# Threading a triangular inverse between tiles of a projection, with its predicated copies over half the columns

## The reference

```
a   = where(strict, (kb @ k.T) * lmask, 0)
t   = triangular_solve(a + eye, eye, lower, unit_diagonal)
u   = t @ (v * beta);   wk = t @ (kb * exp(gc))
# then four chunks in order:
v_new = u_c - w_c @ state
o     = qd_c @ state + a_c @ v_new
state = state * exp(gl_c) + ks_c.T @ v_new
```

## Time and profile before

| | us |
|---|---|
| median of three runs | 1038.01 (1037.69 to 1040.87) |
| the profiled execution, its own time | 1041.72 |
| its span in the profile | 1040.0 |
| PE busy | 1016.9 |
| PE weight loads busy | 934.5 |
| DVE busy | 747.8 |
| ACT busy | 571.0 |
| POOL busy | 70.5 |

### The profile page before, as it was taken

One profiled execution on the slowest core, in us unless ns is written; L12 is line 12 of the kernel. 1 busy time (PEld: TensorE's weight loads), 2 busy tenths in 40 slices (PEclk: granted clock), 3 DMA queues, 4 the chain that ended last, 5 costly groups with the idle time before them and its releaser, 6 DMA issues.

```text
span 1040.0 us, 21726 instructions
## 1 busy us (share of the span) xinstructions
PE 1016.9 (98%) x9135; PEld 934.5 (90%) x9135; DVE 747.8 (72%) x1188; ACT 571.0 (55%) x841; POOL 70.5 (7%) x177
## 2 busy tenths in 40 slices
PE   9999999999999999999999999889999999999997
PEld 8778999999977999999998998779899899998885
DVE  5879677788877966787889967756778566555445
ACT  5775575444666558444468674125345456575333
POOL 8600000000000000011140000000000000000000
PEclk9999999999999999999999998989999999999999
DMA  9656554455664545448787440001355355555652
GB/s 326 178 182 176 153 156 129 145 176 178 196 181 129 154 136 158 126 151 240 160 206 203 123 153 24 24 22 47 118 174 179 126 157 181 178 184 184 196 187 81
DMA packets 73553, 160.57 MB, mean 154 GB/s; under 512 B 6917, under 2 KB 16320, under 8 KB 73456
## 3 DMA queue, kind: packets, MB, share of 16 engines
q1 hardware_dynamic: 70304, 150.59, 46.8%
q0 software_dynamic: 2832, 8.06, 4.0%
q10 hardware_dynamic: 320, 0.53, 0.1%
HBM read 158.11 MB, written 1.05 MB: 153 GB/s over the span
## 4 chain that ended last, share of the span: by engine, by line
PE 86%; DVE 6%; ACT 3%; DMA 2%; issue 2%; ACTq 0%; POOL 0%; DVEq 0%; POOLq 0%
PE psum L470 23%; PE psum L472 22%; PE psum L471 22%; PE psum L883 2%; PE psum L1034 2%; DMA ring<-in_w_in 2%; PE psum L872 1%; DVE ring_lo L1388 1%; PE psum L724 1%; PE psum L702 1%; ACT ring_hi L2446 1%; DMA ring<-in_w_branch 1%; DVE arena L1574 1%; PE psum L1308 1%; PE psum L716 1%
## 5 line engine op out<-in xcount | busy, mean ns | idle before, releaser
L1388 DVE TENSOR_TENSOR ring_lo<-ring,ring_hi 128x1024 fp32r<-128x1024 f32 (+4 forms) x291 | 342.7, 1195 | 174.3 <-ACT ring_hi L2446 172.7
L2446 ACT ACTIVATE ring_hi<-ring 128x1024 fp32r<-128x1024 f32 (+4 forms) x291 | 297.7, 1034 | 268.9 <-PE psum L472 247.4
L470 PE MATMUL psum<-hT,ring_hi 128*128 128x256 f32 x904 | 258.5, 286 | 0.5 <-DVE hT L1748 0.5
L472 PE MATMUL psum<-hT,ring_lo 128*128 128x256 f32 x904 | 255.6, 283 | 0.0
L471 PE MATMUL psum<-hT,ring_hi 128*128 128x256 f32 x904 | 255.2, 282 | 0.0
L470 PEld LDWEIGHTS psum<-hT,ring_hi 128*128 128x128 f32 x904 | 172.4, 191 | 3.0 <-issue 2.4
L471 PEld LDWEIGHTS psum<-hT,ring_hi 128*128 128x128 f32 x904 | 172.4, 191 | 0.0
L472 PEld LDWEIGHTS psum<-hT,ring_lo 128*128 128x128 f32 x904 | 172.4, 191 | 0.0
L470 PE MATMUL psum<-ring_hi,hT 128*128 128x512 f32 (+4 forms) x416 | 156.0, 375 | 1.9 <-DVE ring_lo L1388 1.1
L472 PE MATMUL psum<-ring_hi,hT 128*128 128x512 f32 (+4 forms) x416 | 151.9, 365 | 0.0
L471 PE MATMUL psum<-ring_lo,hT 128*128 128x512 f32 (+4 forms) x416 | 151.6, 364 | 0.0
(11 more groups left out here) (461 smaller groups left out, 1353.5 us busy)
## 6 DMA issues: line engine op xcount, KB each, us to landing
ring<-in_w_in SPq DMA_DIRECT2D x104, 512.0 KB, 3.6
ring<-in_w_ff SPq DMA_DIRECT2D x64, 512.0 KB, 3.5
ring<-in_w_branch SPq DMA_DIRECT2D x24, 512.0 KB, 3.3
ring<-in_w_out SPq DMA_DIRECT2D x24, 512.0 KB, 3.5
ring<-in_w_in SPq DMA_DIRECT2D x24, 384.0 KB, 3.3
ring<-in_w_xkv SPq DMA_DIRECT2D x16, 512.0 KB, 3.8
ring<-in_w_in SPq DMA_DIRECT2D x8, 528.0 KB, 4.1
ring<-in_w_xq SPq DMA_DIRECT2D x8, 512.0 KB, 4.1
```

What stands on the lines that cost most here:

```text
L470: mm(b, lhs[0], rhs[0], start=start, stop=False, **how)
L472: return mm(b, lhs[1], rhs[0], start=False, stop=stop, **how)
L1388: V.tensor_tensor(chunk_view(ring_lo, RAW, c), chunk_view(ring, RAW, c), plain(chunk_view(ring_hi, RING_HI, c)), ALU.subtract).then_inc(ev ...
L2446: AC(chunk_view(ring_hi, RING_HI, c), chunk_view(ring, RAW, c), ACT.Copy).then_inc(ev("whi_ready"), 1)
```

## The change

In TensorE's order the last column projection is issued half a chunk at a time. Its last chunk moves behind the start of the inverse and is split: one half ahead of level 1, the other between the `tx` and the `ty` of level 1. The keys of the memory are issued by tiles (6 matmuls) in place of chunks (24): one tile between `tx` and `ty` of each of levels 2 to 5, one or two after a level, and the last five after the first `state_write`. `memory_states` goes from ahead of level 4 to behind it, `memory_products` from ahead of level 5 to behind it (with two tiles between its parts). `window_scores(0)` goes from behind level 4 to behind `delta_factors`, and `window_scores(1)`, both `window_turns` and the product with the values go into the steps of the delta rule, with `("xk", 1)` by tiles between them.

The orders of DVE and ACT follow. On DVE the masking of the biases moves (one half ahead of level 1, one ahead of level 4), `mlstm_states` goes behind level 4, the maxima go into the delta rule's steps, and `delta_out` and the last `head_norm` come ahead of `window_out`. ACT copies the last column projection behind level 1 and takes the exponentials behind `delta_factors`.

The predicated copies of the levels read and write only the blocks that the mask selects, 192 of 384 columns. For that the mask is kept for three heads. Three small tensors (`own`, `own_eye`, `band`) move to other places, and their making with them.

```diff
-            def T_steps(tag, rhs, tiles=4):
+            def T_steps(tag, rhs, tiles=4, by_tile=False, ready=None):
...
+                        if by_tile and f < tiles - 1:
+                            yield c
...
-            def inverse_level(k):
+            def inverse_level(k, between=None):
...
+                if between:
+                    between()
...
+            last_columns = cols_steps(("p2", 5), hT, by_row=True)
+            for stage in (None, key_products(1), None, query_products, None, inverse_begun):
+                next(last_columns)
+                if stage:
+                    stage()
+            next(last_columns)
...
+            keys = T_steps(("xk", 0), hT, by_tile=True, ready=lambda c: copied(pe, ("memT", c)))
+            inverse_level(1, lambda: next(last_columns))
             memory_turns(2, 3)
             memory_maxima()
             window_heads()
...
+            inverse_level(2, lambda: tiles(keys, 1))
+            tiles(keys, 2)
+            inverse_level(3, lambda: tiles(keys, 1))
             memory_scores()
+            tiles(keys, 2)
+            inverse_level(4, lambda: tiles(keys, 1))
             memory_states()
...
+            tiles(keys, 1)
+            inverse_level(5, lambda: tiles(keys, 1))
             memory_products(0)
+            tiles(keys, 2)
             memory_products(1)
...
             delta_decays()
             delta_factors(0)
             delta_factors(1)
...
+            copied(pe, *[("naT", t, q) for t in range(T) for q in range(2)])
+            window_scores(0)
...
             state_write(0, 0)
             state_write(0, 1)
-            next(keys)
+            run(keys)
             state_read(1, 0)
             state_read(1, 1)
-            next(keys)
+            window_turns(0)
             state_write(1, 0)
             state_write(1, 1)
-            next(keys)
+            window_scores(1)
             state_read(2, 0)
             state_read(2, 1)
-            next(keys)
+            tiles(more_keys, 4)
             state_write(2, 0)
             state_write(2, 1)
...
+            window_turns(1)
             state_read(3, 0)
             state_read(3, 1)
...
+            tiles(more_keys, 4)
...
+            def triangle(ap, k, side):
+
+                w = 2 ** k
+                (p, z, h, n) = [list(d) for d in ap.ap]
+                assert n[0] == 1 and h == [CH, GNH // 2]
+                return bass.AP(tensor=ap.tensor, offset=ap.offset + (0 if side else w),
+                               ap=[p, z, [2 * w, GNH // 2 * CH // (2 * w)], [1, w]])
...
+                        vf(V.copy_predicated(both_triangles(gd_invT[:, t, z, :, :, :], k), both_triangles(level[:, :, k, :, :], k),
+                                             both_triangles(b, k)), free(n))
...
+                    vf(V.copy_predicated(triangle(gd_inv[:, t, d, :, :].rearrange("p (z h) n -> p z h n", z=2), k, d),
+                                         triangle(bc(level[:, d, k, :, :], 1, 2), k, d), triangle(b, k, d)), free(n))
```

The new order of ACT from level 5 on:

```diff
+            inverse_level(5, 0)
+            inverse_level(5, 1)
+            hi_until(42)
+            copy_out("gdec2", stat_all[:, :], 24)
+            delta_factors(0)
+            delta_factors(1)
             act.wait_ge(ev("gdv_ready"), 1)
             window_exp(0, 0)
             window_exp(0, 1)
...
+            hi_until(44)
+            memory_k(0)
+            turned_weights(0)
             full(act, ("nas", 1, 1), 2)
             window_exp(1, 0)
             window_exp(1, 1)
```

More of the change, by code:

```diff
@@ L1096, in _, with inverse_begun @@
-            for t in range(T):
-                filled(moved[t], ("ao", t))
+            def inverse_begun():
+                turn[0] += 6
+                memory_rows()
+                p2_copied(1, 2)
+                for t in range(T):
+                    turns(("mlT", t), [proj2[:, t, C_MLQ + k * P:C_MLQ + (k + 1) * P] for k in range(4)])
+                memory_turns(0, 1)
+                pe.wait_ge(ev("inv0_ready"), 1)
+                for t in range(T):
+                    crossed(("inv0", t), lambda c, odd: (c, c ^ odd, c),
+                            (lambda c, odd, d, p, q: gd_inv[q, t, d, 2 * p + odd, :], lambda c, odd, d, p, q: own_eye[q, :]), lambda d: 1 - d)
+                banks, moved = [open_bank(pe, ("ao", t)) for t in range(T)], {}
+                for swap in range(2):
+                    for d in range(2):
+                        for p in range(GNH // 2):
+                            for t in range(T):
+                                r = CH * (t ^ swap)
+                                o = (d * (GNH // 2) + p) * CH
+                                m = mm(banks[t][CH - r:2 * CH - r, o:o + CH], own_eye[r:r + CH, :], gd_a[r:r + CH, t, d, 2 * p + 1, :],
+                                       start=True, stop=True)
+                                moved[t] = m
+                for t in range(T):
+                    filled(moved[t], ("ao", t))
@@ L1176, in delta_factors, with tiles @@
                     filled(m, ("gw", t, d))
-            inverse_level(1)
+            def tiles(steps, n):
+                for _ in range(n):
+                    next(steps)
+            keys = T_steps(("xk", 0), hT, by_tile=True, ready=lambda c: copied(pe, ("memT", c)))
+            inverse_level(1, lambda: next(last_columns))
             memory_turns(2, 3)
@@ L1215, in _ @@
                 filled(m, ("napv", t))
-            copied(pe, *[(n, t, d) for n in ("gu2", "gw") for t in range(T) for d in range(2)])
             def state_read(j, d):
@@ L2241, in _ @@
             mlstm_keys()
+            dve.wait_ge(ev("zt_ready"), 1)
+            vf(V.scalar_tensor_tensor(out=z2, in0=zt, scalar=1.0, in1=z2, op0=ALU.add, op1=ALU.mult), "dve")
+            copied(dve, *[("naT", t, q) for t in range(T) for q in range(2)])
             scaled_keys(0)
-            lo_until(42)
             inverse_level(3, 0)
```

180 lines of the change are left out of this document (71 added, 109 removed).

## The result

The changed kernel takes 1046.68 us (median of 6 runs, 1043.44 to 1048.93), the kernel before 1038.49 us (6 runs) beside it: a ratio of 1.0075, 95% interval 1.0048 to 1.0101. That is slower by 7.8 us by the ratio, where 1037.1 us was forecast with a range up to 1043.5. A second comparison (8 runs against 24) gave 1044.98 against 1039.88 us, 1.0044 (1.0026 to 1.0063), so 4.6 to 7.8 us are lost; the intervals overlap.

A forecast was written before the change was run, and what follows sets the result against it. TensorE, busy 98% of the span, bounds the kernel; 13.5 us of waits plus 4.6 of clock, 18.1 us lost against 19.0, is 0.9 us faster: median 1037.1 us, range 1030 to 1043.5, no tellable change (0.42).

The forecast's parts named there:

- The stretch: From 604 us to the output projection at 754: TensorE loses 19.0 us before the change, 18.1 us after.
- `ao`: New TensorE wait of 1.2 us for banks DVE releases in `memory_low`, in place of a 0.7 us wait.
- `window_turns(0)`: Delta rule's steps: 2.4 us wait for key banks ACT frees in `memory_k(0)`, with 5 us slow clock.
- the first tile: First tile of `("xk", 1)`, behind `window_scores(1)`: 2.5 us wait for held banks, perhaps 2 us slow clock.
- the group around level 5 and the factors: New waits at `memory_products`, the factors and `window_scores(0)`, behind DVE's work at level 5: 2.2 us counted.
- "issue": TensorE idle without a releaser among the levels' small products: 4.4 us before, half (2.2) taken to stay.
- clock term: Half clock in the stretch after the change: 11.5 us slow (maxima products, `window_turns(0)`, tiles), costing 4.6 us against 6.5.
- price of 0.40: Loss per busy microsecond at half clock, from key matmul spacing: 0.40 us, so 16.2 us cost 6.5.
- Elsewhere: Outside the stretch: bigger mask costs GpSimd time near the start where nobody waits; past 754 orders unchanged. Nothing added.
- The copies: 36 predicated copies of the levels: 0.22 us less each, 8 us less on DVE; TensorE gains only levels' last copies.
- Slower: Rival: the halved clock eats the gain, 20 us slow costing 8.0 and all "issue" left: 1042.7 us, chance 0.22.
- The copies don't get shorter: Rival: level 1's runs of 2 columns cost as much as whole rows; 1040 us, no chance of its own.

The follow-up runs named there:

- run 1: Kernel before with GpSimd's part alone (three-head masks, moved buffers, band ahead of the last bias transfers), whole-width copies, old order: 1044.07 us, ratio 1.0043.
- run 5: Kernel before with three-head masks and moved buffers, band made behind GpSimd's last bias transfers: 1039.78 us, ratio 1.0005.
- run 10: Changed kernel with one edit, the band made behind the last bias transfers; three-head masks still built early: 1042.78 us, ratio 1.0040.
- run 6: Changed kernel with masks built for one head early, and both band and spreading to the other heads behind the bias transfers: 1042.00 us, ratio 1.0020.
- run 7: Kernel before in its old order with narrow copies; one-head masks early, band and spreading behind the bias transfers: 1038.06 us, ratio 0.9975.
- run 8: Changed kernel with GpSimd's band and spreading late, and order repaired on ACT, DVE and TensorE (key tiles ahead of second window scores): 1034.78 us, ratio 0.9945.
- run 11: Changed kernel with GpSimd's band and spreading late, plus only ACT's and DVE's order repairs: 1039.20 us, ratio 0.9993.
- run 12: Changed kernel with GpSimd's band and spreading late, plus only TensorE's order repair (key tiles ahead of the second window scores): 1041.15 us, ratio 1.0020.
- run 3: Changed kernel with one-head masks early, spread by one GpSimd copy ahead of the bias transfers: 1043.62 us, ratio 1.0043.
- run 18: Changed kernel with the band made three times over ahead of the bias transfers: 1048.11 us, ratio 1.0085.

## Why the prediction was wrong

**The stretch.** The sum of the waits for one execution nearly held. Of the 13.5 us of waits forecast 14.6 were found: `ao` 1.1 for 1.2, the second `state_read` 1.3 for 1.1, `window_turns(0)` 1.8 for 2.4, the first tile 2.7 for 2.5; the group around level 5 and the factors 1.6 for 2.2 (three waits of 0.5, 0.4 and 0.7); of the 4.4 us of "issue" 3.1 stayed and not 2.2, and the small ones are 3.0 for 1.9. The waits for `memory_states` and at `memory_products` are gone. The two slow pieces hold 2 x (1 - 0.57) x 4.0 + 2 x (1 - 0.58) x 4.0 = 6.8 us at half clock, 2.7 us lost by the price used, for 4.6. That makes 17.3 against 18.1.

That this total comes near is luck in its clock term, in two ways. The places were wrong: of the three slow pieces that were forecast, only the short one at the first tile is in this profile. The other stands behind a gap of 1.8 us at level 3, which the forecast didn't have, and neither the maxima's products nor `window_turns(0)` is slow:
```profile
656.88 0.21 PE L1030 MATMUL psum<-arena 64*64 64x64 f32 x1 [1.79 <-issue]
```
And the price of 0.40 was wrong for the kernel before. It was read from key products, but the slow pieces there hold many small ones. In the eight profiles of the old order TensorE is busy in the stretch for 132.3 to 136.2 us, with 6.8 to 17.1 us at half clock, which is 0.30 us for each, an estimate by a line through the eight. So the kernel before lost 5.1 us to the clock and not 6.5, and that is why the stretch is only 0.5 us shorter where 17.3 for 19.0 would give 1.7.

**"Elsewhere": the step that failed.** "The bigger mask costs GpSimd time near the start, where nobody waits for it ... nothing in this stretch hangs on it." Nobody waits for GpSimd's result, that is true; but its work has two other ways to TensorE. The large one isn't the mask but the band, which was moved along and which the forecast priced at nothing, without a word: it now runs ahead of bias transfers that GpSimd issues itself. Put behind them, with all else the same, it gives back 3.9 us in the old order (runs 1 and 5) and 0.4 to 3.6 in the new one (run 10). All of GpSimd's part is worth 4.5 us in the old order (run 1), and 2.5 to 5.7 in the new one (the changed kernel's two ratios less run 6's). The term was 0.

The small one is the mask. In the profile its 48 selects take 36.5 us where they took 21.0, and VectorE's operations beside them take longer. Summed up to 100 us, VectorE's operations take 2.0 to 3.0 us more than in the first profile of the kernel before in all nine profiles with the mask built for three heads, and no more (-0.3 to 0.0) in the eleven others. A cast takes 0.32 us and 0.17 before, an operation on two operands 0.28 and 0.16. The first group of the selects, and the two operations:
```profile
L3053 POOL TENSOR_SCALAR_AFFINE_SELECT level<-level 64x96 int8<-64x96 int8 x24 | 18.8, 783 | 1.7
```
```profile
44.73 0.32 DVE L1483 CAST posf<-posi 128x2 f32<-128x2 int32 x1
```
```profile
36.83 0.28 DVE L1393 TENSOR_TENSOR rtmp<-rout 128x4 f32<-128x4 f32 x1
```
In the profile of run 5 TensorE waits 1.5 us longer for splits than before; by the runs it costs 0.5 us (1.9 at most). The Trainium skill ("SBUF — State Buffer", section "Summary: rules for kernel authors") says that when a VectorE instruction has two SBUF inputs while a GpSimd operation reads SBUF, or when it is in a 2-port mode, the second of the two to issue is blocked until the first is done. By that rule the masks lengthen VectorE's work, and the trace agrees as far as the operation on two operands goes; whether the cast was in a 2-port mode no run here shows.

**The base of the sum.** The forecast took the difference of a profiled execution (1041.72 us) and hung it under a median 3.7 us lower. By medians the order with the copies costs 2.1 us (run 6), not a gain of 0.9, and the order alone 4.7 (runs 7 and 6). The profiled executions of the changed kernel (1043.44, 1042.39 and 1045.15 us) lie mostly under its medians, those of the kernel before over theirs (1041.72 and 1041.07 against 1038.0 to 1040.1): by profiles the stretch comes out equal or shorter, by medians longer.

The base was an unusual execution in both of its terms. With whole copies in the old order, six profiles show 12.4 to 14.7 us of waits in the stretch (mean 13.3) and 6.8 to 17.1 us at half clock (mean 11.9); the forecast started from 12.5 and 17. Seven profiles of the new order with the narrow copies, before its repair, show 13.9 to 15.6 us of waits (mean 14.8) and 3.4 to 6.8 us at half clock (mean 5.3). So the waits grow by some 1.5 us. The gain in clock that these profiles show is not in the other executions: the mean clock over all of them is 0.9936 for run 6 and 0.9933 for the kernel before beside it.

The groups of the result point at the clock: a mean clock lower by 0.0055 over 1045 us is 11.5 us more at half clock, 4.6 us at 0.40, and the groups lie 5 us apart. That this time falls in the stretch, behind the new waits, is argued and not shown.

**Which waits the order's loss hangs on.** This is shown. The waits of the delta rule's steps and at `ao` are the ones that the forecast named, and without them the same interleaving takes 7.8 us less (runs 6 and 8) and beats the kernel before by 5.7. The waits themselves are 4.8 us of it (from 6.9 in all to 0.8 and a new one of 1.3). The clock is most of the rest: its mean is higher by 0.0031 in run 8 than in run 6, which at 0.40 is an estimated 2.6 us. Taken one group at a time the repairs give 2.8 and nothing (runs 11 and 12), and the clock is not up by as much (0.9947 and 0.9936). Why it stays up only with both stays open.

**The copies.** 5.7 us less on VectorE (20 x 0.167 + 16 x 0.149) where 8 were forecast: the term failed at level 1 alone, whose eight copies didn't get shorter. That they give TensorE only what the last copies of a level held up was right in kind: 1.5 to 2.6 us in the old order, and in the repaired one 1.0, within the measurement. The forecast gave them no term of their own.

**The rivals.** "Slower" happened, for neither of the reasons costed; the clock in the profile was better than forecast (0.98 for the 0.94 of before), and the part of the loss that GpSimd's work makes was covered by no rival. "The copies don't get shorter" is out for levels 2 to 5 and true for level 1, the one that it named (0.61 us for 0.58).

## What to carry to other kernels

A queue that issues transfers has two kinds of customers: those who wait for its results, and the transfers behind it. When work on such an engine is moved or grows, list what it now stands ahead of, and where those transfers will meet the weights; here 2.9 us of work put in front of five 64 KB transfers cost 3.9 us in the old order beside the masks (1.6 without them), with nobody waiting for its result. When dense work is spread between small dependent steps, check each bank that the dense work holds against the releases of the steps: the interleaving was worth having only after four such releases had been moved ahead (one on TensorE, one on ACT, two on DVE). And a sum against one profiled execution is a forecast for that execution; before it is hung on a median, ask how the clock of that execution stands to the others.

## What the runs showed of the hardware

- At 551 us a wait of 2.0 or 2.3 us was followed, in all three executions that had one (runs 1, 3 and 18), by 3 to 3.5 us at a granted clock of 0.50 or 0.51; the seven waits of 0.8 to 1.7 us in the same place were not. But the wait of 2.7 us at the first tile was followed by the half clock in one of the changed kernel's three executions (715.6 to 719.0 us) and not in the other two. At the product of level 3 named above, an idle time of 1.8 to 3.0 us stands in nine profiles of the new order, and seven of them show the half clock within 2 us behind it; the three with 0.3 to 1.5 us don't. The gap matters, and it doesn't decide alone.
- A predicated copy out of PSUM took 0.58 us for 384 columns in whole rows. For 192 columns it took 0.36 us in runs of 4 to 32 (levels 2 to 5) and 0.60 to 0.62 us in runs of 2 (level 1), in all twelve profiles with narrow copies: leaving out half of the columns gained 0.22 us, and nothing at runs of 2.
- The median landing time of four weight chunks of 408 KB was 3.8 to 5.2 us in the ten profiles with the band elsewhere, and 5.0 to 6.6 us in the ten with the band, or the spreading with it, ahead of the 64 KB transfers of GpSimd's queue. The chunks of other sizes in the same 30 us don't follow: those of 512 KB landed in 4.5 to 5.8 and 4.6 to 5.6 us, those of 384 KB in 4.2 to 5.6 and 3.1 to 3.6. TensorE's wait at 551 us comes some 15 us after the bunch is issued (535.0 us in the changed kernel); that both queues' packets meet in the same DMA engines is the likely reason, and is argued.
